# Products of the identity with itself in TensorE's waits: two joined blocks in f32 precision on one core

## The reference

```python
h = h + jnp.concatenate([o, y], axis=-1) @ w_out[l]
hm = rms_norm(h, g_mlp[l])
h = h + jnp.square(jax.nn.relu(hm @ w_mlp_in[l])) @ w_mlp_out[l]
gate = jax.nn.sigmoid(rms_norm(h, g_ple[l]) @ w_ple_gate[l])
h = h + gate * (p[l] @ w_ple_proj[l])
```

## Time and profile before

| | us |
|---|---|
| median of 3 runs | 2467.65 (2463.88 to 2476.29) |
| profiled execution, own time | 2469.72 |
| its span, first to last instruction | 2467.9 |
| TensorE busy | 2357.4 (96%) |
| VectorE, GpSimd, ScalarE busy | 1428.6, 1425.0, 763.1 |
| mean granted TensorE clock | 0.985 |

### The profile page before, as it was taken

How to read it: one execution, slowest core, us unless ns; L and a number is a source line. 1 busy time by engine, 2 the same in 40 slices (tenths; PEclk the granted TensorE clock), 3 DMA queues, 4 the chain that set the end, 5 groups by cost and what they waited for, 6 DMA issues and landing times.

```text
span 2467.9 us, 33015 instructions
## 1 busy us (share of the span) xinstructions
PE 2357.4 (96%) x12090; PEld 1923.9 (78%) x12090; DVE 1428.6 (58%) x1711; ACT 763.1 (31%) x1612; POOL 1425.0 (58%) x1252
## 2 busy tenths in 40 slices
PE   8989999999998899999998899999999998899998
PEld 6767777888777687788876898998998997676446
DVE  7984311234577541211257787887887888608654
ACT  3343110102231520100126434334334334523451
POOL 8735766767778186667774344344344342165785
PEclk9999999999999999999998999999999999899999
DMA  4211444222213034432233011111011012022112
GB/s 163 92 52 52 144 167 168 94 103 97 99 69 110 10 111 155 170 120 103 102 111 120 35 52 43 42 51 50 35 51 51 34 51 86 28 87 72 39 39 69
DMA packets 35181, 205.06 MB, mean 83 GB/s; under 512 B 4752, under 2 KB 8848, under 8 KB 12176
## 3 DMA queue, kind: packets, MB, share of 16 engines
q1 hardware_dynamic: 27600, 164.85, 19.1%
q10 hardware_dynamic: 7488, 38.87, 4.6%
HBM read 192.44 MB, written 5.24 MB: 80 GB/s over the span
## 4 chain that ended last, share of the span: by engine, by line
PE 75%; DVE 16%; issue 4%; ACT 3%; POOL 1%; DMA 0%; DVEq 0%; SPq 0%; ACTq 0%; POOLq 0%
PE ps L480 38%; PE ps L783 13%; PE ps L1027 5%; DVE convd L2287 3%; PE ps L1144 2%; PE ps L879 1%; PE ps L901 1%; PE ps L1126 1%; DVE convd L2301 1%; PE ps L507 1%; PE ps L918 1%; PE ps L682 1%; PE ps L888 1%; PE ps L1131 1%; PE ps L890 1%
## 5 line engine op out<-in xcount | busy, mean ns | idle before, releaser
L390 POOL TENSOR_SCALAR whi<-wraw 128x512 fp32r<-128x512 f32 x568 | 388.5, 712 | 973.7 <-PE ps L783 441.2
L394 POOL TENSOR_TENSOR wlo<-wraw,whi 128x512 fp32r<-128x512 f32 x568 | 863.0, 1550 | 0.0
L480 PE MATMUL ps<-uhi,whi 128*128 128x512 f32 x896 | 355.1, 396 | 15.5 <-POOL wlo L376 11.1
L480 PE MATMUL ps<-uhi,wlo 128*128 128x512 f32 x896 | 350.0, 391 | 0.0
L480 PE MATMUL ps<-ulo,whi 128*128 128x512 f32 x896 | 349.8, 390 | 0.0
L783 PE MATMUL ps<-inhi,whi 128*128 128x384 f32 (+1 forms) x784 | 243.8, 346 | 6.8 <-DVE inlo L2231 5.5
L783 PE MATMUL ps<-inlo,whi 128*128 128x384 f32 (+1 forms) x784 | 236.6, 336 | 0.0
L783 PE MATMUL ps<-inhi,wlo 128*128 128x384 f32 (+1 forms) x784 | 236.4, 336 | 0.0
L2120 DVE TENSOR_TENSOR h<-h,ps 128x1024 f32<-128x1024 f32 x40 | 48.8, 1221 | 307.5 <-PE ps L480 307.5
L480 PEld LDWEIGHTS ps<-uhi,whi 128*128 128x128 f32 x896 | 168.9, 188 | 58.4 <-POOL wlo L376 11.1
L480 PE MATMUL ps<-hidhi,whi 128*128 128x512 f32 x512 | 201.0, 393 | 0.0
(11 more groups left out here) (452 smaller groups left out, 4652.2 us busy)
## 6 DMA issues: line engine op xcount, KB each, us to landing
wraw<-in_wstream SPq DMA_DIRECT2D x150, 1024.0 KB, 4.8
modraw<-in_modw ACTq DMA_DIRECT2D x24, 1024.0 KB, 4.8
hspill<-hres ACTq DMA_DIRECT2D x1, 3072.0 KB, 9.1
hback<-hspill ACTq DMA_DIRECT2D x1, 3072.0 KB, 9.9
Q<-qrow SPq DMA_DIRECT2D x24, 128.0 KB, 2.3
h<-in_x ACTq DMA_DIRECT2D x2, 1024.0 KB, 5.1
QL<-qrest SPq DMA_DIRECT2D x14, 128.0 KB, 2.3
gw<-in_gates ACTq DMA_DIRECT2D x2, 512.0 KB, 3.6
```

Of the source, the lines that this page charges most:

```text
L390: pool.tensor_scalar(whi[:, s, c], wraw[:, s, c], 1.0, 0.0, ALU.mult, ALU.add).then_inc(wraw_read, 1)
L394: ins = pool.tensor_tensor(wlo[:, s, c], wraw[:, s, c], whi[:, s, c].bitcast(F32), ALU.subtract)
L480: mm = pe.matmul(ps[:, 2 * bank + m, :], a[:, w, c:c + P], b[:, kb, :], start=(n == 0 and i == 0), stop=(n == KB - 1 and i == 2))
```

## The change

A function `busy(n, bank)` issues n products of the 128x128 identity with itself into the first 128 columns of a PSUM bank. Nothing reads them, and each starts its own sum. Twelve batches are executed, 205 products in all.

- V's first tile of layer 0: 24, behind the rate columns and ahead of the wait for the tile's split. The wait for the banks now stands ahead of that for the tile (both layers, both tiles).
- First scores: 22 in layer 0, 40 in layer 1, between the wait for V's first evictions and that for the rotations.
- First seam: 24 ahead of the seventh sum of squares, 9 ahead of the turn, 8 ahead of the spread, 24 ahead of the tile at T_DT.
- Second seam: 4, 8 and 8 ahead of the sixth to the eighth sum of the first half, 6 ahead of the turn, 28 ahead of K's first half.

```diff
@@ -453,6 +453,11 @@
 
             pe.wait_ge(wsplit, l * LAYER_TILES + (k + 1))
 
+        def busy(n, bank):
+
+            for _ in range(n):
+                pe.matmul(ps[:, bank, 0:P], ident[:, :], ident[:, :], start=True, stop=True)
+
         released = [None, None]
 
         def banks_wait(s, read):
@@ -572,8 +577,10 @@
             def values_tile(j):
 
                 w = (l * LAYER_TILES + NFM + j) % 2
+                banks_wait(j, (L["v_r"], l * PER["v_r"] + 2 * j + 2))
+                if j == 0 and l == 0:
+                    busy(24, 0)
                 tile_wait(l, NFM + j)
-                banks_wait(j, (L["v_r"], l * PER["v_r"] + 2 * j + 2))
                 for t in range(4):
                     for kb in range(KB):
                         for i, (a, b) in enumerate(((uhi, whi), (uhi, wlo), (ulo, whi))):
@@ -597,6 +604,8 @@
                     pe.wait_ge(L["v_r"], l * PER["v_r"] + 2 * n + 2)
                 else:
                     pe.wait_ge(L["exp_r"], l * PER["exp_r"] + 2 * (n - 1))
+                if n == 0:
+                    busy(40 if l else 22, 0)
                 pe.wait_ge(L["rope_r"], l * PER["rope_r"] + 8)
                 for c in range(2):
                     q = proj[64 * c:64 * c + 64, Q0 + hd, qb * P:(qb + 1) * P]
@@ -717,14 +726,18 @@
             mm.then_inc(n_ss, 1)
 
         for b in range(KB):
+            if b == 6:
+                busy(24, 7)
             pe.wait_ge(n_sq, SQ_READY[b])
             j = 32 * (b % 4)
             mm = pe.matmul(ps[j:j + 2, 5, :], gf2[:, b, :], hsqr[:, b, :], start=(b < 4), stop=(b >= 4))
         mm.then_inc(n_ss, 1)
+        busy(9, 7)
         pe.wait_ge(L["mod_row"], DEPTH * PER["mod_row"] + 1)
         for c in range(4):
             mm = pe.matmul(ps[:, 4, 2 * c:2 * c + 2], srow[:, c * P:(c + 1) * P], misc[:, 4:6], start=True, stop=True)
         mm.then_inc(L["mod_T"], 1)
+        busy(8, 7)
         pe.wait_ge(n_rs, 2)
         for n in range(2):
             for c in range(4):
@@ -747,10 +760,14 @@
         def half_sums(h):
 
             for j in range(KB):
+                if h == 0 and j >= 5:
+                    busy(4 if j == 5 else 8, 7)
                 pe.wait_ge(n_sq, 8 + KB * h + j + 1)
                 r = 32 * (j % 4)
                 pe.matmul(ps[r:r + 1, 6 + h, 0:HALF], ones[:, 0:1], sqh[:, (KB * h + j) % 6, :],
                           start=(j < 4), stop=(j >= 4)).then_inc(n_ss, 1)
+            if h == 0:
+                busy(6, 7)
             pe.wait_ge(rr_r, 2 + h)
             for c in range(3):
                 mm = pe.matmul(ps[:, h, 400 + c:401 + c], srow2[:, h, c * P:(c + 1) * P], misc[:, 4:5], start=True, stop=True)
@@ -997,6 +1015,7 @@
             mm.then_inc(vt_ps if c < NC - 1 else tile_done, 1)
 
         wait_split(T_ATT)
+        busy(28, 0)
         k_half(0)
         wait_split(T_ATT + 1)
         v_chunk(0)
```

## The result

| | before | after |
|---|---|---|
| median, beside each other on one chip (12 runs each) | 2468.11 (2463.82 to 2476.29) | 2473.26 (2471.08 to 2475.07) |
| profiled execution, own time | 2469.72 | 2471.08 |
| its span | 2467.9 | 2469.1 |
| mean granted TensorE clock of the profiled execution | 0.985 | 0.996 |

The ratio is 1.0019, 95% interval [1.0011, 1.0028]: the change costs about 5 us, a fifth of a per cent. It is within the 0.5% that the forecast called no change, and inside its range, but 3.6 us above its figure of 2469.7; the change costs 5.2 by the medians where +2.0 was forecast. The profiled execution of after is the fastest of its twelve, and that of before was 1.6 above its median, so the two profiles differ by 1.4 us only.

What follows compares the result with a forecast made beforehand. TensorE was taken to bound the kernel almost everywhere (busy 2357.4 of 2467.9 us). Layer 0 +0.5, layer 1 +2.0, first seam +0.3 and second seam -0.8 gave +2.0: 2469.7 us from the median 2467.65, range 2459 to 2477 (8 in 10).

Steps and rivals of the forecast that it cites:

- The price of a product: All batches: each product runs as two matmuls, 0.23 us at full clock and 0.45 at the low one.
- the own sum: Whole run: +0.5 + 2.0 + 0.3 - 0.8 = +2.0 us, 2469.7 us from the median; chance 0.65.
- the first rival: Filling fits the waits: a product costs half, 0.114 us; sum -8.4, 2459 us; chance 0.12.
- The clock is held: Rotations, seams, V's and dt's tiles: products count as activity, so granted clock is 1.00 through all six low stretches.
- The rival of 2511: Products do not hold the clock, so the rest of each batch costs 0.45 a product: about +43 us; chance 0.05.
- The full return: The whole low clock comes back in all those stretches: 27 us, 2441 us; chance 0.04.
- V's tile: Layer 0, V's first tile: starts 2.2 us late, ends at 140.8 in place of 140.2, nobody on the path waits.
- Rotations, layer 0: Layer 0's first scores: 2.6 us late behind 22 products, 2.0 gained back at full clock; sum +0.5 us.
- Rotations, layer 1: Layer 1's first scores: 4.0 us late behind 40 products, less the same 2.0; sum +2.0, the largest term.
- First seam: End of the first block and dt's tile: lateness and faster turn and spread nearly cancel; sum +0.3 us.
- Second seam: Last squares' sums, turn, spread and K: spread sooner, K's 28 products just hidden; sum -0.8 us.
- The fourth rival: Late, with nothing back: clock is held but low clock cost nothing; near +8, 2475.5 us; chance 0.14.

Runs made afterwards that it cites:

- the transposes: Changed kernel with the same full counts, each product issued as a transpose of the identity (one matmul for two): 2466.22 us, ratio 0.9995 against the kernel before.
- the second profile: The changed kernel profiled once more with no edit: 2474.78 us.
- the rotations alone: Changed kernel with only the batches ahead of the first scores (22 in layer 0, 40 in layer 1): 2472.09 us, ratio 1.0022 against the kernel before.
- layer 1's 40 alone: Changed kernel with only the 40 products of layer 1's rotations left: 2472.99 us, ratio 1.0018 against the kernel before.
- the halves: Changed kernel with half the products in every batch, 101 in all: 2465.97 us, ratio 0.9995 against the kernel before.
- the fitted counts: Changed kernel with batches cut to fit their waits (V none; rotations 12, 21; seams 12, 3, 4, 12 and 2, 6, 6, 2, 14): 2467.59 us, ratio 1.0007.

## Why the prediction was right in kind and 3 us short

*The price of a product* (0.23 us, two matmuls) held: 205 products are 410 matmuls, 40 of them took 9.02 us, and 40 more in layer 1 moved the scores by 8.9. This was the dispute between the own sum and the first rival (2459), which needed half the price. What it would have been like the transposes show, at one matmul each: the ratio is 0.9995, not the 0.9966 of its -8.4. Batches of that length gave less than its sum, and in the rotations, which it put at -2.1 and -2.0, they did not hold the clock.

*The clock is held*: 1.00 in all six stretches by the full products, but for 3.4 us behind layer 0's first scores in the second profile. Batches half as long, of products or of transposes, held it at V's tile and the first seam and not in the rotations. The rival of 2511 is gone. (Its term for layer 0 was too small: by 143.24 only 11 of the 22 products would be done, so 11 are left and not 8, near +5 in place of +3.7.) The full return (2441) is gone too.

*V's tile* was to be 2.2 late and cost nothing. It was 2.2 late and ended 0.7 late, 0.5 in the second profile, near the 0.6 predicted, but alone it costs about 3 us by its ratio (0.7 to 5.2). That the lost time stands at the end of layer 0's attention is one profile's word: the same fall stands in a kernel with nothing in layer 0, and in the changed kernel's two profiles that place is free. Why this batch alone cost 3 us is open.

*Rotations, layer 0*: the first scores were put at 145.7 and stand at 145.72. 2.0 was to come back; +2.6 at the scores had become -0.3 by 160 us, so 2.9 did (2.2 in the second profile). The sum of +0.5 reads -0.7 and +0.2 over the stage.

*Rotations, layer 1*: 4.0 late less 2.0. The scores stood at 796.28, 3.0 late, or 3.8 counted from where the stage began; 3.0 came back in both profiles, and up to 805 us the cost is +0.8 and +0.9 in place of +2.0. **The step that failed is the sentence that closes layer 0 and was taken over for layer 1, that later units run at full clock already**, which let the sum end there. In four of four profiles whose first scores of layer 1 ran at the full clock behind 40 products (both of after, the rotations alone, layer 1's 40 alone) the clock fell some 35 us behind them, for 6.8 us, at the attention's end, and that cost 2.8 to 3.0. In the nine profiles with a low stretch of at least 3.4 us at those scores it never did; with 80 products it did not either, though the scores had the full clock. So layer 1's batch costs +3.5 to +3.8, and what was regained at the front is lost behind.

*First seam*: the sums' end, the turn's start, the spread's start and its end were put at 1320.3, 1322.3, 1325.0 and 1327.0. They came at 1322.8, 1324.9, 1327.6 and 1329.4; less the 2.7 with which the stage began, each is within 0.3 of its step. +0.3 was predicted and +0.1 measured, in three of three profiles. But without batches this seam is itself at 0 (six profiles) or at -1.7 (one).

*Second seam*: -0.8 was predicted, +0.9 measured, in four of four. **This is the mis-sized term.** The three sums behind batches were put 0.1, 0.4 and 0.6 late; they were 0.9, 1.4 and 1.9 late (before: 2109.00, 2111.24, 2113.48), or 0.6, 1.1 and 1.6 less the 0.3 with which the stage began. I took 8 products for 1.8 and began them too soon behind the sum: from sum to sum it is 2.72, against the 2.24 in which a square arrives. VectorE in after:
```profile
2118.57 0.18 DVE L2362 RECIPROCAL rcol<-rcol 128x3 f32<-128x3 f32 x1 [2.04 <-ACT rcol L1710]
...
2119.94 1.02 DVE L2387 TENSOR_TENSOR tin<-oacc,ps 128x384 f32<-128x384 f32 x2
2122.10 1.63 DVE L2381 TENSOR_TENSOR inlo<-tin,inhi 128x384 fp32r<-128x384 f32 x1 [1.14 <-ACT inhi L1721]
...
2133.48 0.56 DVE L2381 TENSOR_TENSOR inlo<-tin,inhi 128x384 fp32r<-128x384 f32 x1 [0.88 <-ACT inhi L1721]
```
and before:
```profile
2117.27 0.18 DVE L2343 RECIPROCAL rcol<-rcol 128x3 f32<-128x3 f32 x1 [1.03 <-ACT rcol L1691]
...
2121.51 1.05 DVE L2362 TENSOR_TENSOR inlo<-tin,inhi 128x384 fp32r<-128x384 f32 x1 [1.14 <-ACT inhi L1702]
```
The root of the row comes 1.3 late. The step behind it no longer waits for the spread, which is the 0.8 of the earlier trace rows given back as predicted, and starts 0.6 late, 0.3 less the stage's start. The other 0.6 is the first inlo: 1.63 us where before took 1.05. Beside it stands GpSimd's subtraction for the next weight tile, the same in both:
```profile
2122.05 2.81 POOL L394 TENSOR_TENSOR wlo<-wraw,whi 128x512 fp32r<-128x512 f32 x2
```
In seven of the fourteen profiles the two start within 0.1 us of each other, and inlo takes 1.62 or 1.63: the four with the full batches at this seam, the halves, the fitted counts and the full counts as transposes. In the seven others inlo starts 0.6 behind and takes 1.05 to 1.07. From 2127.87 us in before, behind the end of GpSimd's subtractions at 2126.8, the same operation takes 0.56. GpSimd goes by the end of the spread, VectorE and ScalarE by their own steps, so a sooner spread brings the two together; that their meeting makes inlo longer is what fourteen profiles fit, no run changed it by itself. From there all is 1.2 late to the last inlo, at 2133.48 against 2132.30, for which K's last block waits as before. K's 28 products made the first block 3.1 late and cost nothing, as the step said.

*The sum.* Taking the mean of the two profiles of each kernel: the start +0.3, layer 0 -0.1, layer 1's scores +0.6, the fall behind them +2.8, first seam +1.0, scan -0.4, second seam +1.4, together +5.5; the mean own times differ by 5.6 and the medians by 5.2. Against the one profile from which the forecast was made it would be +1.4, next to the forecast's +2.0. That agreement with its figure is luck: the profiled execution of before was 1.6 above its median and that of after 2.2 below its own. The fourth rival (2475.5, nothing comes back) is nearer in time than the forecast, but its mechanism is refuted by the 2.9 and 3.0.

What is not settled: what makes the clock fall at 831 us or 182 us. The work just ahead of the fall is the same in a profile that has it and one that has not. At 831 us it goes with what happened at the scores 35 us before in 13 of 14 profiles, but that is a count, not a mechanism, and two of the kernels show two kinds of executions, of which one kind each was traced. Nor was it tried to fill the short waits at the end of the attention.

## What to carry to other kernels

Filler for a bound engine must be shorter than the wait that it stands in, priced by executed matmuls and by the distance from one real product to the next: here the full counts cost 5 us and half of them nothing that ten runs could tell, nor did they gain. Low clock is worth only what TensorE does in it on the path; in dt's tile, where VectorE feeds it, a longer stretch of it cost nothing. And where the time hangs on where the clock falls, one profile of each kernel is one draw: compare stages over two profiles of each, and medians of ten runs, before a term of 2 us is believed.

## What the runs showed of the hardware that I had not expected

- Matmuls of the identity keep the clock at 1.00 through the first seam as transposes (0.11 us each) as well as in pairs as products; with batches half as long, of either sort, it fell to 0.50 for 6.8 and 3.4 us in the rotations.
- A stretch kept at full clock went with a fall elsewhere: layer 1's attention ended at 0.50 in four of the four profiles behind a 40-product batch and full-clock scores, in none of the ten others. Why is not shown.
- A subtraction of VectorE (128x384) takes 1.63 us when it starts with one of GpSimd's, 1.05 when it starts 0.6 behind it, and 0.56 behind the end of GpSimd's.
- The same kernel comes in kinds with a different mean clock: 0.987 and 0.989 lie 8 us apart for layer 1's 40 alone, 0.990 and 0.994 lie 4 apart for the fitted counts. The changed kernel, with 0.994 to 0.996 in all twelve, varies by 4.0 us; the kernel before by 12.5 in its twelve, and by 13.7 with 0.983 to 0.987 in its executions beside the experiments.
